# Making x token-major with VectorE's 32x32 transposes and a DRAM round trip, in place of TensorE transposes

## The reference

```python
xbc = jax.nn.silu(causal_dwconv(xbc, conv_w, conv_b))      # x, B and C, each convolved over time
...
xdt = x * dtc[..., None]                                   # needed with tokens on the contracted axis
cb = jnp.einsum("bclgn,bcsgn->bcgls", cc, bc)
y_diag = jnp.einsum("bcgls,bcgrls,bcsgrp->bclgrp", cb, decay, xdt)
states = jnp.einsum("bclgn,bcgrl,bclgrp->bcgrpn", bc, decay_to_end, xdt)
...
y = y + d_skip[..., None] * xs                             # needed with channels on the partitions
```

## Time and profile before

| | |
|---|---|
| median of 3 runs | 1106.47 us (1106.43 to 1106.49) |
| the profiled execution | 1106.54 us, its span 1104.7 us |
| busy | PE 99%, DVE 52%, ACT 43%, POOL 55% |
| TensorE clock | 0.998 |
| DMA | 117 MB, 106 GB/s over the span |

### The profile page before, as it was taken

One profiled execution on the slowest core, in us unless ns is written; L12 is line 12 of the kernel. 1 busy time (PEld: TensorE's weight loads), 2 busy tenths in 40 slices (PEclk: granted clock), 3 DMA queues, 4 the chain that ended last, 5 costly groups with the idle time before them and its releaser, 6 DMA issues.

```text
span 1104.7 us, 15384 instructions
## 1 busy us (share of the span) xinstructions
PE 1092.8 (99%) x5168; PEld 899.8 (81%) x5168; DVE 577.3 (52%) x644; ACT 474.2 (43%) x816; POOL 610.8 (55%) x460
## 2 busy tenths in 40 slices
PE   9999999999999999999999999999999999999997
PEld 7788888888888788888887888888888888888886
DVE  5665421455432384676777866666664124554123
ACT  7433222233333338458595785343332222333332
POOL 3866544444566635537466376656665444445653
PEclk9999999999999999999999999999999999999999
DMA  7223232222222225333334233222222222333232
GB/s 286 79 99 105 86 103 97 96 95 95 96 95 95 96 77 152 123 112 124 117 104 143 105 125 106 96 95 96 95 95 96 95 95 95 97 99 101 93 104 77
DMA packets 40085, 117.05 MB, mean 106 GB/s; under 512 B 4080, under 2 KB 11888, under 8 KB 40048
## 3 DMA queue, kind: packets, MB, share of 16 engines
q1 hardware_dynamic: 39616, 115.83, 31.3%
q10 hardware_dynamic: 432, 0.73, 0.2%
HBM read 114.32 MB, written 2.23 MB: 105 GB/s over the span
## 4 chain that ended last, share of the span: by engine, by line
PE 93%; ACT 2%; DVE 1%; POOL 1%; issue 1%; DMA 1%; ACTq 0%; DVEq 0%; POOLq 0%
PE bank L857 30%; PE bank L859 29%; PE bank L858 29%; PE bank L1048 1%; PE bank L1057 1%; DMA params<-params 1%; ACT m L634 1%; PE bank L898 1%; PE bank L1007 0%; ACT w_hi L445 0%; POOL w_lo L729 0%; POOL residual L756 0%; PE bank L878 0%; PE bank L1025 0%; ACT y_accumulated L609 0%
## 5 line engine op out<-in xcount | busy, mean ns | idle before, releaser
L729 POOL TENSOR_TENSOR w_lo<-w_raw,w_hi 128x512 fp32r<-128x512 f32 x372 | 497.5, 1343 | 442.5 <-ACT w_hi L445 429.9
L445 ACT ACTIVATE w_hi<-w_raw 128x512 fp32r<-128x512 f32 x372 | 230.5, 626 | 383.0 <-PE bank L859 373.5
L857 PE MATMUL bank<-x_hi,w_hi 128*128 128x512 f32 x848 | 331.9, 391 | 1.8 <-DVE x_lo L1159 1.5
L859 PE MATMUL bank<-x_hi,w_lo 128*128 128x512 f32 x848 | 330.2, 389 | 0.0
L858 PE MATMUL bank<-x_lo,w_hi 128*128 128x512 f32 x848 | 330.1, 389 | 0.0
L857 PE MATMUL bank<-act_hi,w_hi 128*128 128x512 f32 (+1 forms) x656 | 252.9, 386 | 0.0
L859 PE MATMUL bank<-act_hi,w_lo 128*128 128x512 f32 (+1 forms) x656 | 251.8, 384 | 0.0
L858 PE MATMUL bank<-act_lo,w_hi 128*128 128x512 f32 (+1 forms) x656 | 251.8, 384 | 0.0
L857 PEld LDWEIGHTS bank<-x_hi,w_hi 128*128 128x128 f32 x848 | 159.2, 188 | 37.5 <-issue 2.8
L859 PEld LDWEIGHTS bank<-x_hi,w_lo 128*128 128x128 f32 x848 | 159.2, 188 | 33.1
L858 PEld LDWEIGHTS bank<-x_lo,w_hi 128*128 128x128 f32 x848 | 159.3, 188 | 32.6
(11 more groups left out here) (161 smaller groups left out, 725.8 us busy)
## 6 DMA issues: line engine op xcount, KB each, us to landing
w_raw<-weights SPq DMA_DIRECT2D x186, 512.0 KB, 3.3
m<-acs_scratch SPq DMA_DIRECT2D x16, 512.0 KB, 4.4
decay_in<-eacs_scratch SPq DMA_DIRECT2D x24, 128.0 KB, 3.8
x_token<-x_tok SPq DMA_DIRECT2D x4, 512.0 KB, 6.4
residual<-xt SPq DMA_DIRECT2D x8, 256.0 KB, 10.1
out_first<-scaled_residual SPq DMA_DIRECT2D x4, 256.0 KB, 2.4
out_second<-output_rows SPq DMA_DIRECT2D x4, 256.0 KB, 2.7
pooling_matrices<-pooling ACTq DMA_DIRECT2D x2, 288.0 KB, 5.2
```

The lines of the kernel that those rows point to most:

```text
L445: act.activation(whi[:, c % 2, part], raw[:, c % 2, part], ACT.Copy).then_inc(hi_ready, 1)
L729: pool.tensor_tensor(wlo[:, c % 2, part], raw[:, c % 2, part], whi_f[:, c % 2, part], ALU.subtract).then_inc(lo_ready, 1)
L857: pe.matmul(out, wh, xh, start=start, stop=False)
L859: return pe.matmul(out, wl, xh, start=False, stop=stop)
```

## The change

The 16 transposes of x of each group leave PE. In their place:

1. The order of a group's six convolution units becomes x, x, x, x, B, C (`conv_cols`, `conv_out`).
2. SiLU of x moves from slot 0 of its group to slot 8 of the group before (`silu_x`; in the lead-in, unit 4).
3. There DVE transposes the four tiles in 32x32 blocks into the free part of `y_accumulated` (`transpose_blocks`, four instructions of 128x512).
4. ACT's queue issues four writes of these blocks to a DRAM scratch in slot 8, after `first_tap` and behind a wait for DVE's transposes (`write_blocks`; each takes 32 partitions, 16 x 128 elements of each, so runs of 512 bytes, 256 KB), and one read of 1 MB in runs of 2 KB at the end of slot 9 behind a wait for the writes (`read_tokens`; group 0: after unit 5, and in slot 0).
5. `token_x` reads the landed x from SBUF in two instructions of 256 elements where one of 512 read PSUM.
6. `skip`, which overwrites the landed x, moves from slot 0 to slot 3 and waits for all four `token_x`.

```diff
+        x_dram = nc.dram_tensor("x_scratch", [GROUPS, CHUNKS * (P // Q), Q, P // Q, GT * Q], F32).ap()
...
-            return bf[:, :] if q == 0 else cf[:, g % 2, :] if q == 1 else xact[:, q - 2, :]
+            return xact[:, q, :] if q < GT else bf[:, :] if q == GT else cf[:, g % 2, :]
...
+            def write_blocks(g):
+
+                act.wait_ge(xt_blocks, g + 1)
+                blocks = x_blocks(g)
+                for a in range(P // Q):
+                    act.dma_start(x_dram[g, :, :, a, :].rearrange("n q f -> q n f"),
+                                 blocks[Q * a:Q * a + Q, :, :]).then_inc(xt_written, 16)
+
+            def read_tokens(g):
+
+                act.wait_ge(xt_written, 16 * (P // Q) * (g + 1))
+                act.dma_start(yx[:, GT * g:GT * g + GT, :],
+                             x_dram[g].rearrange("(c b) q a f -> (b q) c (a f)", c=CHUNKS)
+                             ).then_inc(xt_landed, 16)
+
+            def silu_x(g):
+                act.wait_ge(acc_drained, A_SSM + conv_slot(CONVS * g + GT - 1) + 1)
+                act.activation(xact[:, :, :], xact[:, :, :], ACT.Silu).then_inc(x_act, 1)
...
             def skip(g):
 
-                act.wait_ge(x_act, g + 1)
+                act.wait_ge(xdt_ready, 4 * g + 4)
...
-            def token_x(g, c):
-
-                for i in range(GT):
-                    last = pe.transpose(XT_BANK[c][:, P * i:P * i + P], xact[:, i, P * c:P * c + P], ident)
-                last.then_inc(x_mm, 1)
...
+            def transpose_blocks(g):
+
+                dve.wait_ge(x_act, g + 1)
+                blocks = x_blocks(g)
+                for i in range(GT):
+                    last = dve.transpose(blocks[:, :, Q * i:Q * i + Q],
+                                         xact[:, i, :].rearrange("p (n j) -> p n j", j=Q))
+                last.then_inc(xt_blocks, 1)
...
             def token_x(g, c):
 
-                dve.wait_ge(x_mm, 4 * g + c + 1)
-                dve.tensor_tensor(by_head(xdt[:, c, :]), by_head(XT_BANK[c][:, :]),
-                                  of_group(dt_t[:, :, :].rearrange("p c h -> p (c h)"), c, g, HD), ALU.mult
-                                  ).then_inc(xdt_ready, 1)
+                dve.wait_ge(xt_landed, 16 * (g + 1))
+                if g and c == 0:
+                    dve.wait_ge(yd_ready, 4 * g)
+                    dve.wait_ge(dec_ready, 3 * g)
+                out = xdt[:, c, :].rearrange("p (i h a j) -> p h i a j", h=2, a=2, j=Q)
+                landed = yx[:, GT * g + c, :].rearrange("p (h a i j) -> p h i a j", h=2, a=2, j=Q)
+                dt = dt_t[:, c, HPG * g:HPG * g + HPG].rearrange("p (i h) -> p h i", h=2)
+                for half in range(2):
+                    last = dve.tensor_tensor(out[:, half], landed[:, half],
+                                             dt[:, half].unsqueeze(2).unsqueeze(3).to_broadcast([P, GT, 2, Q]),
+                                             ALU.mult)
+                last.then_inc(xdt_ready, 1)
```

More of the change, by code:

```diff
@@ L56 @@
 TIMES_CB_IN = {4: 1, 6: 2, 8: 3}
-T_TOKEN, T_LATE_TOKEN = 1, 2
+T_TOKEN = 1
+Q = 32
 T_STAT, T_NORM = 4, 7
@@ L256, in build @@
         cb_mm = sem("cb_product")
-        x_mm = sem("x_transposed")
+        xt_blocks = sem("x_blocks_transposed")
+        xt_written = sem("x_blocks_written")
+        xt_landed = sem("x_token_major_landed")
         xdt_ready = sem("x_dt_ready")
@@ L593, in _ @@
                     act.activation(ones_r[:, :], ones, ACT.Copy).then_inc(ones_ready, 1)
+                if u == 5:
+                    write_blocks(0)
             def silu_b_c(g):
-                for q in range(2):
+                for q in range(GT, CONVS):
                     act.wait_ge(acc_drained, A_SSM + conv_slot(CONVS * g + q) + 1)
                     act.activation(conv_out(CONVS * g + q), conv_out(CONVS * g + q), ACT.Silu).then_inc(bc_act, 1)
-            def silu_x(g):
-                act.wait_ge(acc_drained, A_SSM + conv_slot(CONVS * g + CONVS - 1) + 1)
-                act.activation(xact[:, :, :], xact[:, :, :], ACT.Silu).then_inc(x_act, 1)
             def skip(g):
-                act.wait_ge(x_act, g + 1)
+                act.wait_ge(xdt_ready, 4 * g + 4)
                 for i in range(GT):
@@ L659, in _ @@
                     u = slot_of(g, t)
+                    if not ends and t == 8:
+                        silu_x(g + 1)
                     if t == 2:
@@ L664, in _ @@
                         silu_b_c(g)
-                        silu_x(g)
                         if g:
@@ L680, in _ @@
                         first_tap(CONVS * (g + 1) + t - GT)
-                    if t == 0:
+                    if not ends and t == 8:
+                        write_blocks(g + 1)
+                    if not ends and t == 9:
+                        read_tokens(g + 1)
+                    if t == 0 and g == 0:
+                        read_tokens(0)
+                    if t == 3:
                         skip(g)
@@ L1027, in token_major @@
                 last.then_inc(cb_mm, 1)
-                pe.wait_ge(x_act, g + 1)
-                if g == 0:
-                    pe.wait_ge(acsf_ready, 1)
-                else:
-                    pe.wait_ge(y_add, 4 * g)
-                    pe.wait_ge(y_dec, 3 * g)
-                    pe.wait_ge(state_ready, 3 * g)
-                for c in range(CHUNKS - 1):
-                    token_x(g, c)
             def c_chunk(g, c):
@@ L1044, in chunk @@
                 pe.wait_ge(xdt_ready, 4 * g + c + 1)
-                if c:
+                if g == 0 and c == 0:
+                    pe.wait_ge(acsf_ready, 1)
+                else:
                     pe.wait_ge(y_add, 4 * g + c)
@@ L1080, in _ @@
                         token_major(g)
-                    if t == T_LATE_TOKEN:
-                        pe.wait_ge(bt_lo_ready, g + 1)
-                        token_x(g, CHUNKS - 1)
                     if t == T_STAT and g:
@@ L1323, in _ @@
                 conv_scale(u)
+                if u == 4:
+                    transpose_blocks(0)
                 conv_taps(u)
@@ L1467, in _ @@
                         b_token_lo(g)
-                    if t == 3:
-                        token_x(g, 3)
                     if t == T_STAT + 1 and g:
@@ L1504, in _ @@
                         decay_times_cb(g, 0)
+                        token_x(g, 3)
                     if t == T_NORM and g:
```

19 lines of the change are left out of this document (12 added, 7 removed).

## The result

| | median us | runs | ratio to before, 95% interval |
|---|---|---|---|
| before | 1106.48 | 4 (1106.43 to 1106.64) | |
| after | 1122.18 | 4 (1121.33 to 1124.84) | 1.0146 [1.0127, 1.0164] |

The change costs 15.7 us. The forecast was 1109.9, and 1122.2 lies outside its range of 1101 to 1118. The spans of the profiled executions are 1104.7 and 1122.9 us: 18.2 us to explain. The profiled execution of the changed kernel is the slowest of its four (1124.84), so this is more than the difference of the medians.

What follows compares the result with a forecast made beforehand. PE, busy 99%, was taken as the bound. Its 1.68 us saved a group against stalls from ACT's issues and DVE's work gave +0.5, -0.4, +2.0 and +1.3, so +3.4 and 1109.9 us; range 1101 to 1118.

Steps and rivals of the forecast that it cites:

- the wait before chunk 0: PE's wait at the first chunk after the handover: about 0.2 us, in groups 2 and 3 alone.
- 5.6 for `w_lo`: Handovers into groups 2 and 3: ACT's issues delay the weight rounding, so PE stands 2.8 us at each.
- `c_feature`: Group 0: SiLU of C comes late behind transposes and issues, so PE waits 2.2 us before its B transposes.
- What leaves PE's queue is gained in full.: Mamba-2 stage: removing PE's transposes of x saves 1.68 us a group, 6.7 us for four groups.
- rivals B and C: B: issues are cheap, 1102 to 1107 us, chance 0.27. C: all is hidden, 6.7 us come back, 1099.8, chance 0.10.
- about 0.7 us: Group 2: the late skip delays DVE's add of chunk 0; about 0.7 us of it reaches `m` of chunk 2.
- `x_dt` from SBUF: `token_x` in two half-size instructions: nothing to 0.7 us more a chunk, 0.9 us for three in slot 2.
- The transposes, the issues: Slot 8: DVE's four transposes at 0.69 us each, 2.8 in all; ACT's four write issues at 0.9, 3.6 in all.
- Rival D: DVE's transposes are dear, 1.25 us each, adding 2.2 us at each of three places: 1116.6 us, chance 0.14.
- Rival E: The round trip is slow, writes landing after 10.1 us, and x is late for chunk 0: over 1120 us, chance 0.07.
- a sign of being wrong: The forecast is wrong if DVE stands waiting for the landed x in slot 2, which it counted at nothing.
- A slip in the low end: With issues at 0.33 us: -1.7, -0.4, +0.3 and -1.2 for the groups, -3.0 in all, 1103.5 us.

Runs made afterwards that it cites:

- e13: Kernel before, without PE's transposes of x in groups 1 to 3 and without PE's early wait for `b_token_lo` in slot 2: 1105.77 us.
- e6: Kernel before with skip moved to slot 3 and four unused ACT instructions of its size where it stood, in groups 1 to 3: 1106.90 us.
- e3: Kernel before with one edit, skip moved from slot 0 to slot 3, waiting for the four `token_x`: 1112.77 us.
- e17: Kernel before with x convolved ahead of B and C and SiLU of x in slot 8; PE's transposes and skip in slot 0 stay: 1110.98 us.
- e9: Kernel before with `x_dt` formed from SBUF in two halves of 128x256 a chunk instead of from the bank; PE still transposes: 1119.85 us.
- e14: Changed kernel, round trip included, with `x_dt` formed from a bank in one instruction a chunk instead of from SBUF in two: 1122.90 us.
- e1: Changed kernel with the round trip's writes, read and their waits on SP's queue instead of ACT's: 1115.31 us.
- e2: Changed kernel without the round trip's writes and read; DVE forms `x_dt` once its own transposes are done: 1111.88 us.
- e4: Changed kernel with seven unused matmuls keeping PE busy before each chunk 0: 1123.58 us.

## Why the prediction was wrong

The step that failed is the wait before chunk 0. The sum had 0.4 us for it and the trace has 8.7, and the lower clock behind it, 5.1 us, had no term. These two are 13.4 of the 14.8 us by which the profiled execution went past the forecast's +3.4. The other terms nearly cancel: 5.6 for `w_lo` as forecast (in part by luck), 1.3 for `c_feature` instead of 2.2, 1.5 for `x_dt_decayed_lo` instead of nothing.

- **Chunk 0 "about 0.2 us".** 1.6 to 2.9, four times, and the lower clock behind three of them. The working followed the first queue that got late, ACT's weights, and stopped short of three chains to `m`: the landed x and the late loads in group 0, the halves of `x_dt` in groups 1 and 3 (5.1 us each time), and gate, squares, exponentials in group 2.
- **"What leaves PE's queue is gained in full."** It was wrong for the kernel before, and so rivals B and C had the wrong base. PE at 99% with 1.0 us of waits does not say that nothing else is as late. e13 measured 0.6 us for 5.0. The room left was readable: `m` of chunk 2 ended 0.05 us before its use in group 2 and 0.51 in group 1. I used it for chunk 2 of these two groups, and still counted 5.5 of the 6.7 us as gained.
- **The skip and the SiLU of x.** Moved late, the skip was to cost "about 0.7 us" through the adds of y, and slot 0 of ACT was to be the richer. The adds do wait (2.0 us of PE in all), but on the kernel before leaving slot 0 costs 6.4 us for the skip, of which e6 gives 5.9 back (e3), and 4.4 for x first (e17), with POOL's subtractions beside the gate. A hint was in sight: DVE's 1.80 us squares against 0.69.
- **`x_dt` from SBUF.** Counted by its size, 0.9 us for the three chunks in slot 2, over the 1.9 from the banks. Beside POOL the six halves take 6.18 us in e9 and 5.13, 2.09 and 5.14 in groups 1 to 3 of the changed kernel, so in two of the three 3.3 us more and not 0.9. Taking it out (e14) did not lower the time.
- **What held.** The transposes, the issues and the stall on `w_lo` in groups 2 and 3, forecast 2.8 and measured 2.4. ACT's part in the round trip costs 6.9 us (e1), as much as the waits for `w_lo` and `c_feature`; the forecast's stalls from it were 2.2 + 2.8 + 2.8 = 7.8. In group 0 PE waits 1.28 us for `c_feature`; 2.2 was said. Rival D played no part: transposes at 0.62 us.
- **Rival E, and a sign of being wrong.** The writes landed in 4.3 us (median) and not in 10.1, but the read took 8.1, and in group 0 the x was late for chunk 0, as E has it. DVE stood 5.68 us for it in slot 2, which the forecast counted at nothing and named as a sign that it is wrong. PE waited 1.8 us there (2.4 in e1), in the changed kernel behind the late loads of `m` too.
- **A slip in the low end.** With issues at 0.33 us group 2 comes to 2.0 - 2.3 = -0.3 and group 3 to -1.0, not +0.3 and -1.2, so the sum is -3.4 and the low end 1103.1. It does not touch the forecast.
- **The account.** On the changed kernel: ACT's queue 6.9, the rest of the round trip 3.4 (2.4 of them the late x in group 0), and 5.5 without it. e1 and e2 lie so close (1113.9 to 1116.8, 1110.7 to 1113.8) that the last two are good to a microsecond or so. In the last of these are transposes, late skip, order and `x_dt`, whose prices on the kernel before (2.9, 6.4, 4.4, 13.4) are not terms of a sum there: they share one stretch of DVE and POOL, and PE asks later. How the 5.5 us divide among them is open.

## What to carry to other kernels

A bound engine at 99% tells only that it is bound, not by how much; before a saving on it is put in the sum, take the room of the next chain at each place where the two meet, and if the rows show 0.05 us, the saving ends there. Where DVE works with two inputs in SBUF, look at what POOL does at that moment, and count each instruction as one possible wait for a whole POOL instruction: fewer and larger ones, or one operand in PSUM, are cheaper. Work on an engine with time to spare may be what keeps two others apart, so taking it away is a change too, and needs its own price. A round trip needs its price in the first pass, where nothing runs ahead of it, as well as in the steady state.

## What the runs showed of the hardware

- DVE and POOL block each other by instruction: on DVE 128x512 with two SBUF inputs takes 0.68 us alone and up to 1.8 beside POOL, 128x256 takes 0.42 and 1.46; from a bank 128x512 takes 0.68 in either case (e14, 0.679 to 0.692).
- A 32x32 block transpose of 128x512 in fp32 takes 0.67 us on DVE, and four of them 2.48.
- Issuing a write of 512 runs of 512 bytes holds ACT for 0.84 us (median of 16), the read of 2 KB runs for 0.39.
- TensorE's granted clock fell to 1.2 GHz for some 3.4 us behind chunk 0 of groups 1 to 3 of the changed kernel, where PE had waited 1.61, 2.30 and 2.91 us, and not in group 0 behind 1.83 us, behind 2.38 and 2.42 us for `w_lo`, nor in e17 behind 1.7. It stayed at 2.4 GHz behind chunk 0 with PE filled up (e4) and behind the waits of 1.2 us and less in e13. What decides between these the runs do not settle; a low stretch of 3.4 us costs 1.7. In e1 and e2, around waits of 3.3 us in group 2, it lasted some 6.8.
